# The first 52 expert blocks written out on ScalarE, and each low part of the first expert table made by two GpSimd instructions

## What is computed

```
q = (t @ wq).reshape(T, HEADS, 2, QD // 2)
s = einsum('thcd,hcnd->thcn', q, sub_keys); sv, si = top_k(s, 16)
top_s, top_c = top_k((sv[.., 0, :, None] + sv[.., 1, None, :]).reshape(T, HEADS, -1), 16)
experts = take_along_axis(cand_id, top_c);  g = softmax(top_s)
pre = einsum('cd,chkd->chk', x, u_tab[experts])
out = einsum('chk,chkd->cd', gelu(pre) * g, v_tab[experts])
```

## Time and profile before

| | us |
|---|---|
| median of 3 runs | 1203.47 (1202.66 to 1206.82) |
| profiled execution, its time | 1202.06 |
| its span, first to last instruction | 1200.4 |
| granted TensorE clock, mean | 0.98 of full speed |
| PE busy | 1135.0 (95%) |
| DVE, ACT, POOL busy | 823.3, 538.0, 457.7 |
| POOL's low parts, 128 instructions (L588) | 335.4, mean 2.628 |
| first expert pass, first to last block | about 374 to 823 |

### The profile page before, as it was taken

One profiled execution on the slowest core, in us unless ns is written; L12 is line 12 of the kernel. 1 busy time (PEld: TensorE's weight loads), 2 busy tenths in 40 slices (PEclk: granted clock), 3 DMA queues, 4 the chain that ended last, 5 costly groups with the idle time before them and its releaser, 6 DMA issues.

```text
span 1200.4 us, 22934 instructions
## 1 busy us (share of the span) xinstructions
PE 1135.0 (95%) x7693; PEld 1027.9 (86%) x7693; DVE 823.3 (69%) x1825; ACT 538.0 (45%) x959; POOL 457.7 (38%) x243
## 2 busy tenths in 40 slices
PE   7998897898799999999999999999999999999997
PEld 7997675588699998989999999998888888878886
DVE  4446926556699999965666677745666668657666
ACT  4334335333335766765444444443333334334433
POOL 1010325042467999996666666665000003000000
PEclk9999998999899999999999999999999999999998
DMA  6773577335143454444443333344555558445552
GB/s 242 257 278 151 172 247 272 107 105 175 54 140 126 172 175 151 173 166 142 138 140 140 139 133 133 138 150 162 194 193 193 193 192 325 168 156 188 181 193 88
DMA packets 55824, 205.39 MB, mean 171 GB/s; under 512 B 6336, under 2 KB 6336, under 8 KB 55392
## 3 DMA queue, kind: packets, MB, share of 16 engines
q1 hardware_dynamic: 48960, 177.30, 42.7%
q0 software_dynamic: 6528, 27.20, 6.7%
q10 hardware_dynamic: 288, 0.31, 0.1%
HBM read 201.41 MB, written 3.38 MB: 171 GB/s over the span
## 4 chain that ended last, share of the span: by engine, by line
PE 80%; issue 7%; POOL 5%; DVE 5%; ACT 2%; DMA 1%; POOLq 0%; DVEq 0%; ACTq 0%
PE psum L1875 29%; PE psum L1819 9%; PE psum L1814 9%; PE psum L1815 8%; PE psum L1548 5%; PE psum L1849 5%; PE psum L1549 4%; PE psum L1552 4%; POOL w_lo L588 4%; PE psum L1793 1%; PE psum L1751 1%; PE psum L1747 1%; DMA arena<-k_cache_dram 1%; PE psum L1748 1%; PE psum L1532 1%
## 5 line engine op out<-in xcount | busy, mean ns | idle before, releaser
L588 POOL TENSOR_TENSOR w_lo<-ring,w_hi 128x1024 fp32r<-128x1024 f32 x128 | 335.4, 2628 | 115.6 <-ACT w_hi L812 115.3
L1814 PE MATMUL psum<-h_hi,w_hi 128*128 128x272 f32 x1024 | 261.6, 294 | 0.0
L1815 PE MATMUL psum<-h_lo,w_hi 128*128 128x256 f32 x1024 | 255.0, 281 | 0.0
L863 ACT ACTIVATE w_hi<-ring 128x1024 fp32r<-128x1024 f32 x128 | 135.6, 1061 | 215.9 <-PE psum L1875 208.2
L812 ACT ACTIVATE w_hi<-ring 128x1024 fp32r<-128x1024 f32 x128 | 135.5, 1059 | 165.5 <-PE psum L1815 130.6
L1814 PEld LDWEIGHTS psum<-h_hi,w_hi 128*128 128x128 f32 x1024 | 192.8, 188 | 0.3 <-issue 0.2
L1815 PEld LDWEIGHTS psum<-h_lo,w_hi 128*128 128x128 f32 x1024 | 192.9, 188 | 0.0
L1875 PE MATMUL psum<-w_hi,cells_hi 128*128 128x512 f32 x512 | 159.7, 393 | 2.7 <-ACT w_hi L863 2.7
L1407 DVE TENSOR_TENSOR w_lo<-ring,w_hi 128x1024 fp32r<-128x1024 f32 x128 | 157.1, 1227 | 2.8 <-ACT w_hi L863 2.8
L1875 PE MATMUL psum<-w_hi,cells_lo 128*128 128x512 f32 x512 | 158.5, 391 | 0.0
L1819 PE MATMUL psum<-h_hi,w_lo 128*128 128x264 f32 x1024 | 147.2, 286 | 8.8 <-POOL w_lo L588 8.7
(11 more groups left out here) (300 smaller groups left out, 1796.9 us busy)
## 6 DMA issues: line engine op xcount, KB each, us to landing
ring<-experts_u_dram SPq DMA_DIRECT2D x128, 512.0 KB, 3.2
ring<-experts_v_dram SPq DMA_DIRECT2D x128, 512.0 KB, 3.2
ring<-weights_dram SPq DMA_DIRECT2D x78, 512.0 KB, 3.5
arena<-k_cache_dram POOLq DMA_DIRECT2D x16, 576.0 KB, 6.0
arena<-v_cache_dram POOLq DMA_DIRECT2D x16, 512.0 KB, 7.6
kv_out_dram<-arena POOLq DMA_DIRECT2D x1, 2244.0 KB, 8.6
arena<-alibi_dram POOLq DMA_DIRECT2D x1, 1664.0 KB, 8.6
xt<-x_t_dram SPq DMA_DIRECT2D x2, 528.0 KB, 6.0
```

Of the source, the lines that this page charges most:

```text
L588: pool.tensor_tensor(halves_of(w_lo, k, D), raw, halves_of(w_hi, k, D), ALU.subtract)\
L863: act.activation(halves_of(w_hi, k, D), raw, ACT.Copy).then_inc(S["v_hi_made"], 1)
L1814: pe.matmul(out[:, 0:WIDE], part(hi, c, P), h_hi[:, at:at + WIDE], start=(c == 0), stop=False)
L1815: last = pe.matmul(out[:, 0:TP], part(hi, c, P), h_lo[:, at:at + TP], start=False, stop=False)
```

## The change

On ACT the loop over the first 52 blocks becomes written-out code. On POOL the low part is made by two instructions of 512 columns; the first counts up a new semaphore `u_lo_half`, the second `u_lo_made`. PE waits for `u_lo_half` before its first low matmul and for `u_lo_made` before its fifth. All other waits stay.

```diff
             with pool.Fori(0, NK // RING) as i:
                 for k in range(RING):
                     raw, _, _ = expert_tile(i, k)
+                    lo, hi = halves_of(w_lo, k, D), halves_of(w_hi, k, D)
                     pool.wait_ge(S["u_hi_made"], i * RING + k + 1)
 
                     pool.wait_ge(S["u_done"], i * RING + k + 1)
-                    pool.tensor_tensor(halves_of(w_lo, k, D), raw, halves_of(w_hi, k, D), ALU.subtract)\
+                    pool.tensor_tensor(lo[:, 0:512], raw[:, 0:512], hi[:, 0:512], ALU.subtract)\
+                        .then_inc(S["u_lo_half"], 1)
+                    pool.tensor_tensor(lo[:, 512:1024], raw[:, 512:1024], hi[:, 512:1024], ALU.subtract)\
                         .then_inc(S["u_lo_made"], 1)
...
-            with act.Fori(0, BEFORE_ROUTES // RING) as i:
-                for k in range(RING):
-                    high_part(i, k + 2)
-                    gelu(i, k)
+            for b in range(BEFORE_ROUTES):
+                high_part((b + 2) // RING, (b + 2) % RING)
+                gelu(b // RING, b % RING)
...
-                pe.wait_ge(S["u_lo_made"], 2 + i * RING + k + 1)
+                pe.wait_ge(S["u_lo_half"], i * RING + k + 1)
                 for c in range(DC):
+                    if c == DC // 2:
+                        pe.wait_ge(S["u_lo_made"], 2 + i * RING + k + 1)
                     last = pe.matmul(out[:, 0:T], part(lo, c, P), token_part(h_hi, c), start=False, stop=(c == DC - 1))
```

More of the change, by code:

```diff
@@ L138, in build_program @@
             ln_odd q_evac score_filled score_free wq_hi_made wq_lo_made h_hi_made h_lo_made u_hi_made
-            u_hi_used u_lo_made u_done gelu_done route_ready route_exp gates_normed route_filled
+            u_hi_used u_lo_half u_lo_made u_done gelu_done route_ready route_exp gates_normed route_filled
             route_copied iota_placed rows_ready g_filled g_copied g_applied gelu_kept gelu_back cells_made samp_kept h_restored
```

## The result

Over its five runs the changed kernel took 1214.95 us in the median (1210.58 to 1216.32), and 1.0067 of the kernel before, 95% interval 1.0044 to 1.0089. Two further batches of the same kernel gave 1.0063 (1.0031 to 1.0095) and 1.0054 (1.0037 to 1.0072). By these ratios it is slower by some 6.5 to 8 us; the medians of the three batches lie further apart, 11.5, 5.9 and 6.8 us over the kernel before. The forecast of +2.5 us, 1206.0, with 1210.5 as the upper end of its range, was too low. The profiled execution took 1210.58 us, with a span of 1208.9.

A forecast was written before the change was run, and what follows sets the result against it. PE was taken as bound by waits for POOL's low part, 12.0 us lost in blocks 0 to 52. Waits of 14.8 us less 12.3 gave +2.5 us on 1203.47: 1206.0 us, range 1200 to 1210.5.

The forecast's parts named there:

- The bound and what could be won: Blocks 0 to 52: PE waits for POOL's low part alone; 12.0 us are lost, all that the change could win there.
- Price of a half: On POOL, a subtraction of 512 columns takes 1.24 us, a pair 2.48 us, 0.13 more than now.
- The slower rival by a dearer half: POOL's half costs 1.28 us or more: +3.8 us, 1207.3; over 0.3% slower from about 1.275; chance 0.36.
- Turns: In the routing, DVE's waiting operations enter after each POOL half, not each block; PE's waits per full tile 5.0 against 3.8 us.
- the sum: PE's waits in blocks 0 to 52: 0.7, two tiles at 5.0, last 4.1, together 14.8 us; less 12.3 gives +2.5 us.
- The walk: One routing tile laid out by hand: PE waits 1.4, 0.9, 0.7, 0.6 and 0.8 us, together 4.4 us.
- Where the waits fall: In a full routing tile, PE waits at block halves 11b, 13b, 14a, 14b and 16b, 0.6 to 1.4 us each.
- 0.1 more for each restart: On PE, a low part after a wait takes 1.24 us in place of 1.14; raises a tile's 4.4 to 4.9 us.
- The faster rival: POOL's second half keeps DVE out, so turns stay one per block; routing ends about 538.7; about -3 us, 1200.5; chance 0.15.
- Written-out code: ACT's 52 blocks: 25 table loads, 32 us, go, none on PE's path by itself; the longer code costs nothing.
- The routing: On DVE, it ends some 20 us earlier, before 515, and nobody waits for that.
- Chances: Whole kernel: slower by over 0.3% 0.36, within it 0.50, faster about 0.14.

The follow-up runs named there:

- c2: Changed kernel with PE's first 52 blocks written out and 20 extra matmuls in the long pause of blocks 14, 27 and 40: 1.0028 of the kernel before, median 1209.08 us.
- a2: Kernel before with only ACT's loop over 52 blocks written out, low part in one instruction: 0.9975 of the kernel before.

## Why the prediction was right and where it failed

- **The bound and what could be won:** right. 12.0 us were said to be lost in blocks 0 to 52; without collisions the pass is 11.9 us shorter (165.5 to 153.6).
- **Price of a half:** right. 1.24 us was taken, and halves that do not wait follow each other at 1.23 to 1.26 us, with few exceptions. The rows that it was worked out from the earlier trace rows are additions in the code, not subtractions; the price held all the same. The slower rival by a dearer half is out: its condition, over 1.275, is not met.
- **Turns:** right in kind, and 0.7 us short in the sum. The 15 halves that collide take 2.98 to 3.44 (about 3.3 forecast), L1334 shrank to 3.27 (3.3 forecast). The walk gave 4.4 us of waits for a full tile in five pauses of 0.6 to 1.4. Where the clock does not fall (c2), the first tile has 1.37 at block 11, the filled pause of some 2.5 at block 14 and 0.57 at block 17: 4.4 us. The pass of 169.0 is 3.5 us over before; the sum said 14.8 - 12.0 = 2.8 for it (the 0.3 us of block 0 lie ahead of the pass and came: 2.3 to 2.1). Where the 0.7 us lie was not traced.
- **Where the waits fall:** wrong. The walk had the second pair of long operations hit 13b and 14a. POOL was half a block further, and both hit block 14. Three pauses of 0.9, 0.7 and 0.6 became one of 2.5.
- **The step that failed:** "0.1 more for each restart". A pause was priced by its length and this 0.1, because the pauses before, all up to 1.2 us, cost no more. The pause of 2.5 us also cost the clock: 3.41 us for 2.01 in the next high part and 0.06 in its low part, 1.46 us. Some is given back, since PE then comes later to the small wait at block 17 (0.57 us in c2, none in the first changed execution). Net by the passes: 169.0 with no fall, 171.3 with two, 172.3 with three, so about 1.1 us each. +3.5 and three times 1.1 are the 6.8 us of the first execution. So a term that the sum put at nothing, the clock behind a pause, was worth 3.3 us.
- **The faster rival** is refuted for this change: DVE was let in between the two halves of a block. Its own sum was good: a2 has its conditions but for the start on a half, and there the pass was 2.6 us shorter (3 said) and PE met the routing at block 52, as said.
- **Written-out code:** its 32 us of ACT's time were on nobody's path, as said. That it alone would bring 2.6 us stands only in the faster rival, not in the forecast. As part of the change it brought nothing.
- **The routing:** it ended at 519.2, 138.8 us behind the first low matmul (154.5 before); "before 515" was missed mostly by the later start of block 0 (with the earlier one it would have been 515.4). Counted from the first low matmul it came 15.7 us sooner, not some 20. Nobody waits for it, as said.
- **Chances:** the chance of 0.36 for slower was put on a dearer half alone, so that slower came true by another cause is luck. No rival had a merged pause that the clock answers, though one long wait per tile was within half a block of the walk. That is why the range ended too low.

## What to carry to other kernels

Splitting an instruction that takes turns with another engine handed that engine an extra turn at each cut; ask first whether the collision itself can go, here by one input in PSUM, which was worth 10 us where the split cost 7. When a schedule laid out by hand gives several pauses close together, also price the case that they fall into one, with the clock's answer in it. To tell a clock loss from a wait, fill the pause with idle work: if more work takes less time, it was the clock.

## What the runs showed of the hardware

- Pauses of PE of 2.08 to 2.52 us inside this dense pass were followed by the half clock for some 3.4 us in 11 of 14 cases (five executions); the other pauses of all passes in the table, 0.16 to 1.64 us, in none. The same pause of the same kernel (2.44 to 2.48 us at block 14) was answered in two executions and not in a third. The Trainium skill, TensorE: Matmul & The Clock Gate, section "HAM oscillation — how this bites in real kernels", tells of waits for DMA of about 3 to 5 us between bursts of matmuls that send the clock to its lower level each time; here pauses of 2.1 to 2.5 us were enough, though not each time.
- Back-to-back instructions of POOL, the second with no wait, do not keep DVE out: L1336 went in between the two halves of block 14.
- A table load that the loop repeated cost ACT 1.3 us each, and written out it stands once.
